# Moving the residual's matmuls ahead of the routing counts in a two-block transformer kernel

## What is computed

```
x = x + g1 * y                                   # the residual: x stays as the base of the sum
h2 = modulate(x, norm2_g, sh2, sc2)
gp = softmax(h2 @ w_rg + b_rg);  g_w, g_idx = top_k(gp, 1)           # one of 4 groups
el = (h2 @ w_re + b_re).reshape(t, 4, 8);  el_sel = el[g_idx]
e_w, e_loc = top_k(softmax(el_sel), 2)                               # two of its 8 experts
for each expert e and its tokens:  ys = (silu(xb @ w1[e]) * (xb @ w3[e])) @ w2[e]
x = x + g2 * (sum over a token's experts of weight * ys)
return rms_norm(x, norm_f_g)
```

## Time and profile before

| what | value |
|---|---|
| time, median of 3 runs | 1613.78 us (1613.31 to 1615.56) |
| time of the profiled execution | 1616.89 us |
| its span, first to last instruction | 1615.1 us |
| TensorE busy | 1417.7 us, 88% |
| VectorE busy | 639.5 us, 40% |
| ScalarE busy | 523.7 us, 32% |
| moved by DMA | 395.05 MB |
| expert loads | 192 of 1024 KB, median 22.5 us from issue to landing |

### The profile page before, as it was taken

How to read it: one execution, slowest core, us unless ns; L and a number is a source line. 1 busy time by engine, 2 the same in 40 slices (tenths; PEclk the granted TensorE clock), 3 DMA queues, 4 the chain that set the end, 5 groups by cost and what they waited for, 6 DMA issues and landing times.

```text
span 1615.1 us, 24943 instructions
## 1 busy us (share of the span) xinstructions
PE 1417.7 (88%) x10476; PEld 1052.1 (65%) x10476; DVE 639.5 (40%) x1232; ACT 523.7 (32%) x975; POOL 59.0 (4%) x52
## 2 busy tenths in 40 slices
PE   6998999999999999989999999998897676676664
PEld 3653476888888887746899998898753333333332
DVE  4336445333333344574655666677421101101101
ACT  4425524322122222644643446455310000000001
POOL 1000013000000001201000000000000000000000
PEclk9999999999999999999999999999898878877878
DMA  9974951524322242654757357335799999999996
GB/s 375 378 277 140 303 209 52 196 72 135 113 75 72 74 155 104 251 179 170 258 175 235 109 193 259 129 131 184 278 422 422 423 423 423 424 424 424 423 424 271
DMA packets 168556, 395.05 MB, mean 245 GB/s; under 512 B 11620, under 2 KB 124792, under 8 KB 142584
## 3 DMA queue, kind: packets, MB, share of 16 engines
q1 hardware_dynamic: 167720, 391.91, 64.3%
q10 hardware_dynamic: 720, 1.49, 0.3%
HBM read 392.32 MB, written 1.05 MB: 244 GB/s over the span
## 4 chain that ended last, share of the span: by engine, by line
PE 69%; DMA 20%; ACT 4%; DVE 4%; issue 2%; SPq 1%; POOL 0%; DVEq 0%; ACTq 0%; POOLq 0%
DMA R<-in_w_dram 18%; PE ps L906 14%; PE ps L912 14%; PE ps L907 14%; PE ps L2746 4%; PE ps L606 3%; PE ps L928 2%; PE ps L929 2%; PE ps L934 2%; PE ps L2795 2%; DMA R<-in_w_ada_dram 1%; PE ps L1222 1%; PE ps L2824 1%; PE ps L1279 1%; PE ps L1253 1%
## 5 line engine op out<-in xcount | busy, mean ns | idle before, releaser
L875 DVE TENSOR_TENSOR WL<-R,WH 128x1024 fp32r<-128x1024 f32 (+1 forms) x202 | 226.5, 1135 | 210.6 <-ACT WH L865 210.6
L2746 PE MATMUL ps<-R,XG 128*32 128x256 f32 x2048 | 173.3, 497 | 118.6 <-DMA R<-in_w_dram 112.2
L906 PE MATMUL ps<-HH,WH 128*128 128x256 f32 (+2 forms) x872 | 273.0, 335 | 0.3 <-ACT WH L865 0.3
L907 PE MATMUL ps<-HL,WH 128*128 128x256 f32 (+2 forms) x872 | 270.0, 330 | 0.0
L865 ACT ACTIVATE WH<-R 128x1024 fp32r<-128x1024 f32 (+1 forms) x202 | 191.1, 961 | 153.0 <-PE ps L912 117.1
L2746 PEld LDWEIGHTS ps<-R,XG 128*32 128x32 f32 x2048 | 86.8, 136 | 198.0 <-issue 181.0
L906 PEld LDWEIGHTS ps<-HH,WH 128*128 128x128 f32 (+1 forms) x872 | 164.4, 188 | 23.7 <-issue 6.5
L907 PEld LDWEIGHTS ps<-HL,WH 128*128 128x128 f32 (+1 forms) x872 | 164.8, 189 | 16.7
L912 PE MATMUL ps<-HH,WL 128*128 128x256 f32 (+2 forms) x872 | 164.5, 330 | 0.0
L906 PE MATMUL ps<-GH,WH 128*128 128x512 f32 (+1 forms) x480 | 153.7, 339 | 0.1
L907 PE MATMUL ps<-GL,WH 128*128 128x512 f32 (+1 forms) x480 | 153.5, 339 | 0.0
(11 more groups left out here) (481 smaller groups left out, 1719.5 us busy)
## 6 DMA issues: line engine op xcount, KB each, us to landing
R<-in_w_dram SPq DMA_DIRECT2D x192, 1024.0 KB, 22.5
R<-in_w_ada_dram SPq DMA_DIRECT2D x72, 1024.0 KB, 7.0
R<-in_w_gate_up_dram SPq DMA_DIRECT2D x40, 1024.0 KB, 7.1
R<-in_w_in_dram SPq DMA_DIRECT2D x20, 1024.0 KB, 8.4
R<-in_w_down_dram SPq DMA_DIRECT2D x16, 768.0 KB, 4.4
R<-in_w_down_dram SPq DMA_DIRECT2D x16, 640.0 KB, 4.4
R<-in_w_in_dram SPq DMA_DIRECT2D x8, 512.0 KB, 7.4
R<-in_w_out_dram SPq DMA_DIRECT2D x16, 256.0 KB, 4.0
```

Of the source, the lines that this page charges most:

```text
L875: last = e.tensor_tensor(L, w, H.bitcast(F32), ALU.subtract)
L906: e.matmul(b[0:n, 0:N], H[:, k, 0:n], xh(k, N), start=(k == 0), stop=False)
L907: e.matmul(b[0:n, 0:N], H[:, k, 0:n], xl(k, N), start=False, stop=False)
L2746: mm = e.matmul(PS[4][32 * g:32 * g + 32, 0:256], x[:, 4 * hf + k, :], w[g // 2][:, k, 256 * (g % 2):256 * (g % 2) + 256], start=(hf == 0 ...
```

## The change

The residual goes into the banks before the counts and no longer after them. `pe_router` now calls `pe_residual` first. That function goes through banks 0 to 3: for each it waits until ScalarE has made its two copies out of the bank, clears the bank and puts in x's two k-tiles. After banks 1 and 3 it raises `s_rtp`. The three later users of `s_rtp` count in the new order, and the two rooms on XT now wait for 2 and 3. The second call after the first gather is gone. No matmul is added or dropped.

```diff
-            (oG, (s_mm, N_TILES)), (oX, (s_rtp, 4)), (oX + 8 * KB, (s_rtp, 5)))
+            (oG, (s_mm, N_TILES)), (oX, (s_rtp, 2)), (oX + 8 * KB, (s_rtp, 3)))
...
-        e.wait_ge(s_rtp, 2)
+        e.wait_ge(s_rtp, 4)
         e.activation(G8T[:, :], PS[7][0:8, 0:128], ACT.Copy).then_inc(s_g2, 1)
...
-        e.wait_ge(s_rtp, 3)
+        e.wait_ge(s_rtp, 5)
         e.activation(G2Q[:, :], PS[6][:, 0:256], ACT.Copy).then_inc(s_g2, 1)
 
     def pe_router(e):
+        pe_residual(e)
         pe_counts(e)
...
         last.then_inc(s_rtp, 1)
+
+    def pe_residual(e):
+
         e.wait_ge(s_zero, 1)
-        e.wait_ge(s_rta, 8)
-        for j in range(4):
-            e.matmul(PS[j][:, :], ZERO[:, 0:128], ZERO[:, :], start=True, stop=False)
-        pe_residual(e, 0)
-
-    def pe_residual(e, h):
-
-        for k in range(4 * h, 4 * h + 4):
-            for a in range(2):
-                col = 256 * a + 128 * (k % 2)
-                last = e.matmul(PS[k // 2][:, col:col + 128], XT[:, k, 128 * a:128 * a + 128], ident, start=False, stop=False)
-        last.then_inc(s_rtp, 1)
+        for g in range(4):
+            e.wait_ge(s_rta, 2 * g + 2)
+            e.matmul(PS[g][:, :], ZERO[:, 0:128], ZERO[:, :], start=True, stop=False)
+            for k in (2 * g, 2 * g + 1):
+                for a in range(2):
+                    col = 256 * a + 128 * (k % 2)
+                    last = e.matmul(PS[g][:, col:col + 128], XT[:, k, 128 * a:128 * a + 128], ident, start=False, stop=False)
+            if g % 2:
+                last.then_inc(s_rtp, 1)
...
         if X is X0:
             pe_first_gather(e)
-            pe_residual(e, 1)
```

## The result

The changed kernel took 1619.59 us (median of 8 runs, 1617.65 to 1621.95) against 1614.59 us for the kernel before (8 runs, 1613.31 to 1619.43). The ratio is 1.0027 with a 95% interval of 1.0018 to 1.0036: slower by 5.0 us, or 0.3%. (The ratio is an estimate over all runs and not the quotient of the two medians, which is 1.0031 here; the two can differ by 0.1% in the experiments too.) The forecast was 1613.0 us, range 1610.6 to 1615.5. It is missed on the slower side, to which I had given 0.04.

A forecast was written before the change was run, and what follows sets the result against it. The prediction took the experts as bound by the weight stream. Gain 0.6 plus 0.15 from expert 0's earlier start, about 0.8 us, took the median 1613.78 to 1613.0 us, range 1610.6 to 1615.5: no difference that can be told.

The forecast's parts named there:

- The bound and the formula: Expert stage: bound by the weight stream at 423 GB/s; gain at the first load into a used room is 0.6 - s.
- Everything turns on s: Expert 0's start, shifted by s against 1161.24: forecast s = -0.15, ends -1.9 and +1.6 us.
- The clock of the gather: First gather, after TensorE idles nearly 4 us: half the records at half clock, 5.28 us; wholly slow 7.04 us.
- Residual against the copies: Residual behind ScalarE's copies: 1.15 us a bank at full clock, ending at 1148.25, so the counts start 0.85 us late.
- The counts: Router counts after the residual: full clock, 1.25 us to VectorE's read at 1149.5, 0.3 us earlier than before.
- A: First gather wholly under the half clock after the pause: loss 1.0 us, 1614.8 us; chance 0.2.
- B: Residual: TensorE falls behind ScalarE's copies at half clock, gather fast; s = +2.7, loss 2.1 us, 1615.9 us; chance 0.08.
- The sign that did show: Expert 0's start: before 1159 or after 1163 would show the prediction wrong; forecast start 1161.1.
- C: DMA stream around the XT loads: both holes gained, no new one opens; gain 4.3 us, 1609.5 us; chance 0.05.
- D: XT loads: something else holds them, so the change does nothing for the stream; 1613.8 us; chance 0.05.
- That leaves 0.9 us: no hole: Stream behind expert 0's first four ring loads: next load moves at 1173.4 + s, before they end at 1174.3 + s.
- What follows takes about 13 us in every case: End of the kernel: the work after the last load it waits for takes about 13 us, whatever the case.

The follow-up runs named there:

- 15 zeros: The changed kernel plus 15 zero matmuls (128x512, bf16) in TensorE's pause ahead of the first gather; 1617.70 us, ratio to the kernel before 1.0004.
- zeros in both pauses: The changed kernel plus 7 zero matmuls ahead of the residual and 15 ahead of the first gather; 1613.53 us, ratio to the kernel before 0.9981.
- half of the residual: The changed kernel with banks 2 and 3 of the residual moved behind line 2472, into the pause before the gather, no zeros added; 1616.59 us, ratio 1.0004.
- zeros in three places: The changed kernel plus zero matmuls: 7 ahead of the residual, 15 ahead of the first gather, 5 behind it; 1612.56 us, ratio 0.9990.
- without the 7 ahead: The changed kernel plus 15 zero matmuls ahead of the first gather and 5 behind it, none ahead of the residual; 1613.55 us, ratio 0.9987.
- half with zeros: The changed kernel with residual banks 2 and 3 behind line 2472, plus zero matmuls: 7 ahead, 6 behind bank 3, 5 behind the gather; 1612.62 us, ratio 0.9989.
- wide in the gather: The changed kernel plus two 512-column zero matmuls behind each k-tile of the first gather (16 in all), none elsewhere; 1619.55 us, ratio 1.0023.
- zeros in the old order: The kernel before, its order kept, plus 21 zero matmuls between the raw logits and the counts; 1613.35 us, ratio 0.9987.
- late rooms: The changed kernel with residual banks 2 and 3 behind line 2472, 7, 6 and 5 zero matmuls, and XT rooms released by the gather; 1612.89 us, ratio 0.9988.
- one wait for all copies: The changed kernel with zeros in three places (20 ahead of the residual), the residual waiting once for all eight ScalarE copies; 1614.81 us, ratio 0.9999.

## Why the prediction was wrong

Point by point, by its own steps:

- **The bound and the formula** held, with one repair. I wrote "Gain = 0.6 - s" with s the shift of expert 0's start, and took the first room to come free a fixed 1.86 us behind that start. Measured, s is +3.4 and the formula gives a loss of 2.8 us where the stretch lost 5.75: the first room came free 3.7 us behind the start, since expert 0 began at half clock (1.7), and the stream lost 1.2 more. With s read at the first load into a used room instead, the formula gives the stretch to the last landing within 0.45 us in seven of the eight traces that have the XT loads early and end on a load, the change itself being the exception:

| run | s | 459.7 - gain | measured |
|---|---|---|---|
| 15 zeros | 0.0 | 459.1 | 459.3 |
| zeros in both pauses | 0.0 | 459.1 | 459.45 |
| half of the residual | -0.8 | 458.3 | 458.2 |
| zeros in three places | -1.6 | 457.5 | 457.9 |
| without the 7 ahead | +1.25 | 460.35 | 460.1 |
| half with zeros | -2.3 | 456.8 | 456.6 |
| wide in the gather | +3.5 | 462.6 | 463.05 |
| the change | +5.1 | 464.2 | 465.45 |

- **"Everything turns on s"** was right, and s was wrong: -0.15 forecast, +3.4 at expert 0's start and +5.1 at the first used room.
- **"The clock of the gather"** is the step that failed. I took "half of the records at each level", 5.28 us, and as the worst end a gather wholly at half clock (7.04 us); it took 7.07, so the worst end is what came. Two things were missing from that end. I let TensorE recover by the time of expert 0, as if any work lifted the level; the gather's 64-column matmuls did not, and expert 0 began at half clock too: 5.57 us, 1.7 later at its first free room. And I added nothing for the slow banks of the residual. That this pause was the danger, the prediction had said; how much of the gather it would slow, it had only split down the middle. The strict reading of the Trainium skill's rule (TensorE: Matmul & The Clock Gate, "What's actually happening") that stood beside the sum had the right sign; the trace agrees with it in the pause (0.50 from 1154.2 on).
- **"Residual against the copies"**: I took the full clock. It fell at 1143.9, banks 0 to 2 took 1.65, 2.13 and 1.36 us, and the residual ended 8.0 us after the raw logits, not 6.1. In two of the other runs (15 zeros, wide in the gather) it ended at 6.3. In the seven traces with no zeros behind the raw logits, the level fell soon after these in four (0.75, 1.0, 2.4 and 2.5 us after their end) and not in three. So this term varies between executions, and one trace cannot price it.
- **"The counts"**: 1.07 us from the residual's end to VectorE's read, 1.25 forecast; the read came 1.4 us late and not 0.3 early, wholly from the residual's late end.
- **Rivals A and B** were both half right, and both together had only a part of the 0.04. B names the place of the second loss and says "the gather is at full clock" because TensorE "has then worked for long"; the trace refutes that, since the pause before the gather is there in either case. A and B together, plus expert 0's slow start, give the result. B's mark for when it would cost time was also worked out wrongly: by its own terms s = 0.6 is reached when the residual ends at 1149.6 with slow counts or 1150.75 with fast ones, not at 1150.5 with slow ones. On that scale it ended at 1150.1, with fast counts. The sign that did show is the one for expert 0: a start after 1163 (it would be 1164.6 there). C and D are out: one hole stayed, and the XT loads did go early.
- **"That leaves 0.9 us: no hole"** was wrong too. The windows show 310 GB/s at 1179 to 1183, four microseconds in which 1.1 us of work at 423 GB/s is missing. That is about the 1.2 us by which the formula misses the change itself; no run was made for it alone, so its cause stays open.
- **"What follows takes about 13 us in every case"**: 13.2 to 14.2 us from the last landing to the end of the span in the twelve traces that end on a load, 13.3 in both kernels. It did not matter for the change, but it blurs the comparison of single executions by up to 1 us.

What stays open: the scatter hides differences of a microsecond, so the order of the versions between 1612.5 and 1613.6 us is not settled, and why zeros in the old order lower the median while their trace looks like that of before is not either. The same holds for zeros in both pauses and for the run without the 7 ahead of the residual: 459.45 and 460.1 us to the last landing, against 459.7, and medians 1.4 to 1.7 us lower. Five of them have intervals wholly below 1 against the kernel before (0.9981, 0.9987, 0.9989, 0.9988 and 0.9987), so by the measured times there are versions faster than both, by some 2 us against before and 6 to 7 against the change. For the 2 us the traces show a cause only in the two runs with half of the residual and zeros (456.6 and 457.4 us to the last landing).

## What to carry to other kernels

Work that stands in front of a critical step may be what keeps TensorE's clock up, or brings it up; before moving it, ask what TensorE does in the microseconds it leaves, and price the step behind at half clock, with the step after that one too. Where a pause must be, a few wide matmuls of zeros are cheap cover (27 of them turned 1619.6 us into 1612.6). And when the next room of a stream is freed by compute, an earlier load only moves the hole: work out the gain at the first load that waits for something else.

## What was not expected of the hardware

- A gather of 64-column f32 matmuls kept TensorE busy for 7.06 us at 0.50 without a rise; with 512-column matmuls between its pieces it rose 4.9 us after the gather began. At full clock, the same gather followed by 1.38 us of pause was followed by a fall in two runs. A pause of 1.2 us between the residual's 128-column matmuls and the counts was not followed by a fall in two runs where zeros stood ahead of the residual (half of the residual with zeros, and the same with late rooms), and was in the one where none did (half of the residual: pause 1.14 us, fall 1.9 us after its end). In the order of before, with 21 zeros and then 0.73 us of pause, the level fell 2.0 us after the pause's end.
- The end of the raw logits lies between 1138.2 and 1145.0 us in the thirteen profiled executions, with the same program up to there. Within one kernel the runs scatter by 3.4 to 9.9 us; a good part of that can thus arise ahead of everything that was changed, though only one execution of each kernel was traced.
- In one profiled execution (one wait for all copies, 1620.51 us against a median of 1614.81) the chain near the end has TensorE idle for nothing that the profile shows:

```profile
1580.08 3.69 issue
1583.77 1.07 PE ps L2753 x7
1584.84 4.33 issue
```

With it, the end is no longer set by the last landing. In the changed kernel one such piece of 2.4 us lies at 1582.3, on the chain but covered by the load behind it; five other traces have one of 2.4 to 3.1 us in the same place, covered too. What TensorE does in them is not shown.
